# Two of tile 0's expert heads moved to the 8 KB rows, all late queries of tiles 1 to 3 spread over eight heads, and a quarter of those heads' value rows added by VectorE

## The reference, cut to what matters

```python
h   = x + W_out [ FoX(8 heads) || DiffAttn(4 heads) ]( W_in RMSNorm(x) )   # SEQ 512, D_MODEL 1024
hn  = RMSNorm(h)
# PEER, per token and head (8 heads):
q   = (hn @ w_q).reshape(tokens, 8, 2, 128)
sc  = einsum('thpd,hpkd->thpk', q, sub_keys)         # 2 x 128 key scores
s1, i1 = top_k(sc[:, :, 0], 16);  s2, i2 = top_k(sc[:, :, 1], 16)
top_s, pos = top_k(s1[..., :, None] + s2[..., None, :], 16)
eidx = (i1 * 128 + i2) at pos                        # 16 of 16384 experts
g   = softmax(top_s)
hid = gelu(einsum('thkd,td->thk', u_tab[eidx], hn)) * g
out = RMSNorm_final(h + einsum('thk,thkd->td', hid, v_tab[eidx]))
```

## Time and profile before

| | |
|---|---|
| median of 3 runs | 1575.78 us (1573.56 to 1581.61) |
| profiled execution, its time | 1577.52 us |
| its span, first to last instruction | 1575.3 us |
| VectorE busy | 1139.9 us (72%) |
| TensorE busy | 1260.2 us (80%) |
| moved by DMA | 594.92 MB |
| mean granted clock of TensorE | 0.916 of full |

### The profile page before, as it was taken

One profiled execution on the slowest core, in us unless ns is written; L12 is line 12 of the kernel. 1 busy time (PEld: TensorE's weight loads), 2 busy tenths in 40 slices (PEclk: granted clock), 3 DMA queues, 4 the chain that ended last, 5 costly groups with the idle time before them and its releaser, 6 DMA issues.

```text
span 1575.3 us, 12952 instructions
## 1 busy us (share of the span) xinstructions
PE 1260.2 (80%) x3685; PEld 659.3 (42%) x3685; DVE 1139.9 (72%) x2676; ACT 443.6 (28%) x1062; POOL 767.2 (49%) x650
## 2 busy tenths in 40 slices
PE   9986998987685846989987768687777877777777
PEld 7665564566452523444433323233332333333233
DVE  3247889999999887666676677667666676666664
ACT  3332234444443212212222222221222222222222
POOL 0025657776575673444554444444453454555440
PEclk9997998998887877999999989989999998999999
DMA  9378989998888899999999999999999999999995
GB/s 380 144 284 325 383 323 348 360 364 330 275 289 323 309 382 387 420 421 422 421 422 421 422 422 422 421 421 422 422 421 421 422 422 421 421 422 421 421 422 209
DMA packets 101613, 594.92 MB, mean 378 GB/s; under 512 B 11688, under 2 KB 11688, under 8 KB 46248
## 3 DMA queue, kind: packets, MB, share of 16 engines
q0 software_dynamic: 92160, 536.91, 84.9%
q1 hardware_dynamic: 9384, 57.19, 9.2%
HBM read 591.96 MB, written 2.10 MB: 377 GB/s over the span
## 4 chain that ended last, share of the span: by engine, by line
DMA 34%; DVE 13%; PE 13%; ACT 2%; POOL 2%; issue 2%; POOLq 0%; DVEq 0%
PE acc L934 11%; DMA mix_mem<-in_peer_uv_dram,eidx 8%; DMA map_mem<-in_peer_uv_dram,eidx 7%; DMA v_ring<-in_peer_uv_dram,eidx 6%; DMA v_all<-in_peer_uv_dram,eidx 4%; DMA u_ring<-in_peer_uv_dram,eidx 3%; DMA act_mem<-in_peer_uv_dram,eidx 3%; DMA w_ring<-in_peer_uv_dram,eidx 3%; PE mm L728 1%; DVE v_all L1465 1%; DVE map_mem L1465 1%; DVE v_ring L1465 1%; DVE u_ring L1465 1%; ACT diag L1118 1%; DVE mix_mem L1465 1%
## 5 line engine op out<-in xcount | busy, mean ns | idle before, releaser
L644 POOL DMA_INDIRECT u_ring<-in_peer_u_dram,eidx x128 | 158.0, 1234 | 197.1 <-DVE gneg L1442 98.8
L1111 ACT ACTIVATE gel<-hid 128x4 f32<-128x4 f32 x126 | 25.8, 205 | 742.7 <-DVE hid L1465 698.6
L651 POOL DMA_INDIRECT v_ring<-in_peer_v_dram,eidx x128 | 152.3, 1190 | 72.0 <-issue 33.2
L934 PE MATMUL acc<-v_all,diag 128*128 128x512 f32 x240 | 118.3, 639 | 64.1 <-ACT diag L1118 64.1
L1493 DVE SCALAR_TENSOR_TENSOR h<-v_ring,coef,h 128x1024 f32<-128x1024 f32 x128 | 164.3, 1283 | 5.9 <-DMA v_ring<-in_peer_v_dram,eidx 2.6
L1457 DVE CUSTOM_DVE_ANT_0 u_ring<-u_ring,hn 128x1024 f32<-128x1024 f32 x128 | 156.1, 1219 | 10.7 <-DMA u_ring<-in_peer_u_dram,eidx 10.2
L934 PE MATMUL acc<-u_ring,diag 128*128 128x512 f32 x240 | 121.3, 653 | 27.8 <-ACT diag L1118 27.8
L934 PE MATMUL acc<-v_ring,diag 128*128 128x512 f32 x240 | 118.6, 641 | 30.2 <-ACT diag L1118 30.2
L934 PE MATMUL acc<-map_mem,diag 128*128 128x512 f32 x240 | 116.1, 629 | 28.2 <-ACT diag L1118 28.2
L1118 ACT ACTIVATE diag<-ident,coef 128x128 f32<-128x128 f32 x376 | 121.1, 390 | 30.6 <-DVE coef L1483 21.5
L728 PE MATMUL mm<-act_mem,w_ring 128*128 128x384 f32 x352 | 126.8, 519 | 2.6 <-issue 1.9
(11 more groups left out here) (264 smaller groups left out, 2346.5 us busy)
## 6 DMA issues: line engine op xcount, KB each, us to landing
w_ring<-in_slabs_dram SPq DMA_DIRECT2D x37, 1024.0 KB
v_ring<-in_slabs_dram SPq DMA_DIRECT2D x6, 1024.0 KB, 10.7
u_ring<-in_slabs_dram SPq DMA_DIRECT2D x4, 1024.0 KB, 10.9
h<-in_x_dram SPq DMA_DIRECT2D x4, 512.0 KB, 6.9
u_ring<-in_peer_u_dram,eidx POOLq DMA_INDIRECT x128
v_ring<-in_peer_v_dram,eidx POOLq DMA_INDIRECT x128
out_dram<-fin SPq DMA_DIRECT2D x3, 512.0 KB, 7.8
w_ring<-in_first_halves_dram SPq DMA_DIRECT2D x2, 512.0 KB, 4.6
```

Of the source, the lines that this page charges most:

```text
L644: nc.gpsimd.indirect_dma_start(out=u_ring[:, c % U_RING, :], out_offset=None, in_=peer_u[0], in_offset=bass.IndirectOffsetOnAxis(ap=eidx[n ...
L651: nc.gpsimd.indirect_dma_start(out=v_ring[:, c % V_RING, :], out_offset=None, in_=peer_v[0], in_offset=bass.IndirectOffsetOnAxis(ap=eidx[n ...
L934: last = nc.tensor.matmul(acc[half][:, :], diag[:, c % COLS, :], v_row(n, c)[:, half * BANK:(half + 1) * BANK], start=first, stop=(n % PH ...
L1111: nc.scalar.activation(gel[:, par, g0:g0 + COLS], hid[:, par, g0:g0 + COLS], ACT.Gelu).then_inc(gelu_done, 1)
```

## The change

- `HOST_HEADS = 6`: heads 0 to 5 are hosted, heads 6 and 7 of tile 0 are late rows, summed in `acc`. `SLOTS` is 24 and the pieces are dealt over all of it. VectorE's two memsets of `acc` go; TensorE starts the sum itself, after the hosted pieces' banks are emptied.
- All 16 queries and 8 keys of tiles 1 to 3 are late pieces: `LATE_EVERY = 4`, behind the first, second and third group of late heads 6 to 13 (32 groups, 128 rows). The ring has ten places up to late row 142 instead of 94.
- In these 128 rows every fourth (`VECTOR_ROW = 3`) is added to `h` by VectorE (`add_late`) and gets no diagonal; it is counted by `v_added`.
- GpSimd's first gathers into three places get waits of their own: place 0 (`v_all`) for the last attention product, place 8 (tile 0's key scores) for head 7's `topk_first`, place 9 (`mix_mem`) for the last `mixT`. SP loads the last four slabs behind tile 0's output instead of the last two.

```diff
-HOSTS = 1
+HOST_HEADS = 6
-LATE_HEADS = 4
-LATE_EVERY = 5
+LATE_EVERY = 4
+VECTOR_ROW = 3
...
+        if g > 0:
+            return ps
         queries = []
-        for hd in range(PH if g == 0 else PH - LATE_HEADS):
+        for hd in range(PH):
...
-    SLOTS = HOSTS * PH * GRP
+    SLOTS = HOST_HEADS * GRP
...
-        k = int(at / total * (SLOTS - 1) * GAPS)
+        k = min(SLOTS * GAPS - 1, int(at / total * SLOTS * GAPS))
...
+    for hd in range(PH):
+        for step, p in enumerate((("query", g_late, 2 * hd), ("query", g_late, 2 * hd + 1), ("keys", g_late, hd))):
+            LATE_PE[LATE_EVERY * hd + step] = p
+            LATE_COPY[LATE_EVERY * hd + step + 1] = p
+    LATE_GROUPS = LATE_EVERY * PH
...
+        KEYS_ROW, MIX_ROW = RING - 2, RING - 1
+        FULL_FROM = LATE_GROUPS * COLS + FULL_RING
...
+        def by_vector(r):
+            return HOSTED <= r < HOSTED + LATE_GROUPS * COLS and r % COLS == VECTOR_ROW
...
             for t in range(TILES - 1):
                 if t == 1:
-                    for n in range(len(slab_order) - 2, len(slab_order)):
+                    for n in range(len(slab_order) - 4, len(slab_order)):
                         load_slab(n)
...
                 if lap > 1:
-                    pool.wait_ge(v_used, HOSTED + place_rows[place][lap - 2] + 1)
+                    last = HOSTED + place_rows[place][lap - 2]
+                    if by_vector(last):
+                        pool.wait_ge(v_added, added(last))
+                    else:
+                        pool.wait_ge(v_used, used(last))
+                elif place == 0:
+                    pool.wait_ge(pv_done, len(item_list))
                 elif place == EARLY_ROWS:
                     pool.wait_ge(dot_done, HOSTED)
                     pool.wait_ge(v_used, HOSTED)
+                elif place == KEYS_ROW:
+                    pool.wait_ge(topk_step, TK * (PH - 1) + TK_FIRST)
+                elif place == MIX_ROW:
+                    pool.wait_ge(mm_full, mm_done(("mixT", GROUPS[-1][-1], 1)))
...
+                    if by_vector(r):
+                        continue
+                    first = (n % PH == 0 or n == HOST_HEADS) and c == 0
+                    if first and n == HOST_HEADS:
+                        pe.wait_ge(*emptied(MM[MM_HOSTED - 1]))
...
+            def add_late(n, par, c):
+                r = TOPK * n + c
+                dve.wait_ge(coef_done, GRP * n + c // COLS + 1)
+                if added(r) > 1:
+                    dve.wait_ge(v_added, added(r) - 1)
+                else:
+                    dve.wait_ge(v_used, HOSTED)
+                ht = h[:, n // PH, :]
+                nc.vector.scalar_tensor_tensor(out=ht, in0=v_row(n, c), scalar=coef[:, par, c:c + 1], in1=ht,
+                                               op0=ALU.mult, op1=ALU.add).then_inc(v_added, 1)
...
-                for half in range(2):
-                    link(nc.vector.memset(acc[half][:, :], 0.0))
-            for n in range(PH * HOSTS, HEADS):
+            for n in range(HOST_HEADS, HEADS):
...
                     coefs(n, par, grp * COLS)
+                    if by_vector(TOPK * n + grp * COLS + VECTOR_ROW):
+                        add_late(n, par, grp * COLS + VECTOR_ROW)
                     if n % PH == 0 and grp == 0:
                         fin_tile(t - 1)
```

More of the change, by code:

```diff
@@ L277, in build @@
     g_late = len(GROUPS) - 1
[L278 to L284, removed]
+    LATE_PE, LATE_COPY = {}, {}
+    for hd in range(PH):
[3 more added lines that the diff above has]
+    LATE_GROUPS = LATE_EVERY * PH
+    assert LATE_GROUPS <= GRP * (2 * PH - HOST_HEADS)
     ORDER = HOSTED_PIECES + [LATE_PE[k] for k in sorted(LATE_PE)]
@@ L316, in build @@
     mm_no = {name: i for i, name in enumerate(MM)}
-    MM_HOSTED = mm_no[("keys", PH - LATE_HEADS - 1, GROUPS[-1][-1])] + 1
+    MM_HOSTED = mm_no[("query", g_late, 0)]
     xs_no, xs_prev, reader = {}, {}, None
@@ L546, in slab_view, with added, used @@
             return w.rearrange("p (c n) -> p c n", c=KC)
-        HOSTED = HOSTS * PH * TOPK
+        HOSTED = HOST_HEADS * TOPK
+        def by_vector(r):
+            return HOSTED <= r < HOSTED + LATE_GROUPS * COLS and r % COLS == VECTOR_ROW
+        vector_rows = [r for r in range(HEADS * TOPK) if by_vector(r)]
+        tensor_rows = [r for r in range(HOSTED, HEADS * TOPK) if not by_vector(r)]
+        tensor_no = {r: i for i, r in enumerate(tensor_rows)}
+        def added(r):
+            return sum(v <= r for v in vector_rows)
+        def used(r):
+            return r + 1 - added(r)
         def row_place(n, c):
@@ L569, in build @@
         TK = 25
+        TK_FIRST = 11
         TK_IDX = 22
@@ L675, in _ @@
                 gather_u(0, c)
-            for n in range(PH * HOSTS):
+            for n in range(HOST_HEADS):
                 for c in range(TOPK):
@@ L921, in peer_group @@
                 for c in range(g0, g0 + COLS):
-                    first = n % PH == 0 and c == 0
-                    if first:
+                    r = TOPK * n + c
[4 more added lines that the diff above has]
+                        pe.wait_ge(*emptied(MM[MM_HOSTED - 1]))
+                        pe.wait_ge(*emptied(next(u for u in reversed(MM[:MM_HOSTED]) if u[0] not in ON_SCALAR)))
+                    elif first:
                         pe.wait_ge(acc_drained, 2 * (n // PH))
@@ L943, in _ @@
                 piece(*p_)
[L944 to L950, removed]
+            for n in range(HOST_HEADS):
+                for grp in range(GRP):
+                    for gap in range(GAPS):
+                        for p_ in pieces_in(n, grp, gap):
+                            piece(*p_)
+            for n in range(HOST_HEADS, HEADS):
                 for grp in range(GRP):
                     peer_group(n, grp * COLS)
-                    k = GRP * (n - PH * HOSTS) + grp
+                    k = GRP * (n - HOST_HEADS) + grp
                     if k in LATE_PE:
@@ L1115, in peer_group @@
                 act.wait_ge(coef_done, GRP * n + g0 // COLS + 1)
[L1116 to L1119, removed]
+                for c in range(g0, g0 + COLS):
+                    if not by_vector(TOPK * n + c):
+                        diagonal(n, par, c)
             def peer_last(n, par, g0):
@@ L1154, in _ @@
             gate_exp(0)
[L1155 to L1167, removed]
+            for n in range(HOST_HEADS):
+                for grp in range(GRP):
+                    for gap in range(GAPS):
+                        if gap == 2 * COLS - 2:
+                            gelu(n, n % 2, grp * COLS)
+                        for p_ in pieces_in(n, grp, gap):
+                            piece(*p_)
+                    if grp == 2:
+                        gate_exp(n + 1)
+            for n in range(HOST_HEADS, HEADS):
                 for grp in range(GRP):
@@ L1620, in _ @@
-            for n in range(PH * HOSTS, HEADS):
+            for n in range(HOST_HEADS):
+                par = n % 2
+                for grp in range(GRP):
+                    k = GRP * n + grp
+                    behind = ((k - 1) // GRP, (k - 1) // GRP % 2, (k - 1) % GRP * COLS)
+                    for gap in range(GAPS):
+                        c = gap // 2
+                        if grp == 1:
+                            topk_second(n + 1, 1 - par, gap)
+                        elif gap == GAPS - 1:
+                            next_head(n, par, grp)
+                        if gap % 2 == 0 and gap < GAPS - 1:
+                            dot(n, par, grp * COLS + c)
+                        elif gap < GAPS - 1 and k > 0:
+                            if c == 0:
+                                coefs(*behind)
+                            add_row(behind[0], behind[1], behind[2] + c)
+                        for p_ in pieces_in(n, grp, gap):
+                            piece(*p_)
@@ L1621, in _ @@
+            coefs(n, par, grp * COLS)
+            for c in range(COLS):
+                add_row(n, par, grp * COLS + c)
+            for n in range(HOST_HEADS, HEADS):
                 t, par = n // PH, n % 2
```

76 lines of the change are left out of this document (29 added, 47 removed).

## The result

The changed kernel takes 1584.75 us (median of 21 runs, 1579.74 to 1590.33) against 1577.73 for the kernel before in as many (1573.40 to 1582.81): ratio 1.0044, 95% interval 1.0034 to 1.0054, 7.0 us slower. Forecast was 5.3 us slower, 0.34%, told as no change on its slow side. The profiled execution took 1579.74 us.

A forecast was written before the change was run, and what follows sets the result against it. Engines, mostly VectorE, were taken to set the hosted part, and DMA at 422 GB/s the late part. +89.5 - 93.9 + 10.7 - 1.0 = +5.3 us, 1581 us on the median's scale; range 1561 to 1594, likeliest 1574 to 1589.

The forecast's parts named there:

- Late part +89.5 us: Late part: 32 more rows and four more query slabs at 2.486 us each, if DMA stays full.
- Hosted part, VectorE's work: -93.9: Hosted part: 56.1 us of bare rows, three groups (29.8) and one search (8.0) go, if VectorE sets the pace.
- the 28th group's first dot: Hosted part, 526.55 us: from here only rows, queries and keys of tiles 1 to 3 left; 61.4 us go.
- the 5.3 us of pending adds: End of hosted part: four adds of the group before remain, 1.283 each with their coefficients, leaving 56.1 us saved.
- Lost to TensorE: +10.7: Hosted stretches set by TensorE, where removing rows saves nothing; 6.7 in the first projections; bounds 6.7 and 20.
- Border -1: Border of hosted and late parts: earlier second group against a new gather wait, net -1 us, bounds -3 and +3.
- Late waits 0: Late part: waits for keys 0 (bounds 0 and +12), border of tiles 0 and 1 0, at most 3.
- VectorE alone as the hosted bound: Rival, hosted part: the lost 10.7 us don't appear and VectorE's idle shrinks; about 1561 us; chance 0.28.
- TensorE as the bound of the whole: Rival, hosted part: TensorE's chains allow only 84% busy, hosted part 402 long, sum +17, 1592 us; chance 0.19.
- A late part that is not full: Rival, late part: the keys' wait or the ten places cost 8 to 12 us on top, 1591 us; chance 0.10.
- the 1.65 us of the gather at 621.18: Late part: GpSimd's gather, 0.94 us with VectorE idle; trace would allow blocking by VectorE; 2.486 us available per row.

The follow-up runs named there:

- run 3: Changed kernel with tiles 1 to 3's 16 column projections cut to half their contraction: ratio 0.9983 to the kernel before.
- run 5: Changed kernel with each hosted value row added on 512 of its 1024 columns only: ratio 0.9900 to the kernel before.
- run 6: Kernel before with each hosted value row added on 512 of its 1024 columns only: ratio 0.9841 to the kernel before uncut.
- run 1: Changed kernel with no value row on VectorE, TensorE summing all 16 rows of each late head with queries: 1581.52 us, ratio 1.0033 to the kernel before.
- run 4: Kernel before with tiles 1 to 3's 16 column projections cut to half their contraction: ratio 0.9998 to the kernel before uncut.
- seven hosted heads: Changed kernel with seven hosted heads instead of six and the first head's queries of tiles 1 to 3 hosted again: 1567.93 us, ratio 0.9955 to before.

## Why the prediction was right

The form was right: (end of the hosted part) + (late bytes at full rate). Point by point:

- **Late part +89.5 us.** The rate is 419 to 422 in every slice from 512 us to the last but one; nothing speaks against the term.
- **Hosted part, VectorE's work: -93.9.** Measured 35.2 (VectorE's work gone ahead of the last norm2) + 64.4 (time gone after it, 68.4 - 4.0) = 99.6 us. My border at the 28th group's first dot cut 12.6 us behind the last norm2, and I took back only the 5.3 us of pending adds; the term was 5.7 too small.
- **Lost to TensorE: +10.7.** Measured 35.2 - 22.8 = 12.4, with bounds of 6.7 and 20 given. In the first projections it was 7.1 + 0.2, forecast 6.7: this is the step that the mechanism carried. The other 5 us lie elsewhere than I had put them: from the first map to the third attention half nothing was lost (forecast 2, bound 0), since TensorE's clock rose with its density as the bound had assumed, but 3.1 in the seventh stretch (forecast 0) and 2.6 in the first (forecast 1); the other three are within 1.6 of either sign. TensorE as the cause is shown for the first projections alone, which run 3 shortens from 54.1 to 48.8 us. In the first and seventh it is not, and it is unlikely: TensorE is busy 23 of 41 and 44 of 67 us there. That the sums agree (12.4 and 10.7) is in part luck.
- **A later start, not forecast.** The first dot came at 110.34 us, before at 108.5, though nothing ahead of it was changed. Five of the six profiles with six hosted heads have it at 109.4 to 110.5 and run 5 at 107.5; the others have it at 107.3 to 108.7. The cause is open, and it may be mere variation.
- **Net of the hosted part:** 99.6 - 12.4 - 1.8 = 85.4 us, forecast 83.2.
- **Border -1.** The 3.5 us of lost transfer at 600 to 640 are gone (rate 420), some 0.5 us at 500 to 540 came (rate 416): -3, my bound.
- **Late waits 0.** Right: keys 0.3 us, the border of tiles 7.4 us of TensorE under a full rate. A gather takes GpSimd 1.20 to 1.41 us on the mean, by place, from 531 to 860 us, with a row's 2.486 to spend.

The sum of the measured terms is 89.5 - 85.4 - 3 = +1.1, the two profiled executions differ by 2.2 us, the medians by 7.0. The profiled execution of the changed kernel was 5.0 us under its median, that of before 0.2. So some 5 us of the difference stand in no profile here; I can't say in which stretch the usual execution spends them. The terms, as far as a profile shows them, add up to 4 us less than forecast, and these 5 us make up for it: that the forecast came within 2 us of the medians' difference is in part luck; its form is not.

*The rivals.* VectorE alone as the hosted bound: refused by runs 5 and 6 (44% and 37% come back). TensorE as the bound of the whole: refused by run 3, whose stretches behind the first projections kept their length whether TensorE was busy 7.8 us less or 2.5 us longer. A late part that is not full: refused by the rate and run 1. What none of them had is DMA as a near bound of the hosted part, shares of 0.96 in the second and fourth stretch of the kernel before, 0.99 in run 6, and VectorE's waits for rows in runs 4 and 6. That fits the kernel before gaining nothing from run 4, while the changed kernel, with fewer 4 KB rows (0.86), gained 9.6 from the same cut.

*VectorE and the gathers.* The prediction left open whether the 1.65 us of the gather at 621.18 came from VectorE. The traces decide it. The VectorE operation in which that gather began, in the kernel before:

```profile
620.79 1.22 DVE L1465 CUSTOM_DVE_ANT_0 v_all<-v_all,hn 128x1024 f32<-128x1024 f32 x1
```

The dot ends at 622.01, the gather at 622.83, 0.82 us later. So it is all through the late part: in the changed kernel 152 of 402 gathers from 530 us on begin while a row's dot is under way, and 150 of them end 0.80 to 0.83 us after the dot, whatever was left of it, so that they last 0.94 to 1.99 us. The other two began within 0.05 us of the dot's start and took 0.93 and 0.94. So did the gather at 595.93 in the kernel before, beside which the prediction called VectorE idle: a dot began there in the same instant. The 12 gathers begun during an operation with one input, such as a reduction or an index search, took 0.93 or 0.94 too. Nine gathers began in one of the 32 new adds and lasted up to 1.46, in all some 4 us of GpSimd's time; it cost nothing that could be seen, as each gather had 2.486. The Trainium skill has this as a rule (SBUF — State Buffer, "SBUF: two separate sides"): a VectorE operation with two SBUF inputs and a GpSimd operation that reads SBUF exclude each other, and whichever starts first holds the shared port pair to its end. The trace agrees, as dots and adds have two SBUF inputs and a gather reads its expert numbers `eidx` from SBUF.

*Where the change goes wrong* can be told in groups of four rows. From the kernel before to seven hosted heads, four hosted groups were worth 57.3 us and cost 47.2 late: gain. From seven to six, the next four (and one head of queries) were worth 28.1 us (525.1 to 497.0) and cost 42.3 late: loss of 14, which is what the ratios show (0.9955 to 1.0044). The first four groups took three heads' queries with them and left the density at 18.4 shares; taking the second four squeezed the same attention pieces into fewer groups.

## What to carry to other kernels

When work is moved from a part set by engines to one set by DMA, the moved bytes have a fixed price as long as DMA stays full, while what they free depends on what stands beside them: cut both traces at the same pieces and compare each stretch's busy times, DMA share and waits, since a stretch whose other engine is full gives nothing back. A move that pays for the first unit can lose on the second; try the amounts one by one. And where two other resources are nearly full, taking work from one returned only 0 to 44% of it here.

## What the runs showed of the hardware

- In run 6 the hosted rows of 4 KB came at 384 GB/s with the DMA engines at a share of 0.99, the late rows of 8 KB at 421 to 422 at 1.01: 388 against 417 GB/s per busy share. This is no fixed price of the smaller rows: run 4 reached 411 at 1.02 from 160 to 190 us, with 4 KB rows and slab loads between.
- A gather that GpSimd begins while VectorE runs a dot or an add of two SBUF tensors ends 0.80 to 0.83 us after that operation: 0.93 to 0.94 us alone, up to 1.99 behind a dot of 1.22.
- TensorE's granted clock fell when products were left out: in the fourth stretch it was 0.96, and 0.86 in run 3; so products worth 41 us at full clock took only 17.5 us off TensorE's busy time.
